# Eight experts per turn of TensorE's loop, and each upper bound loaded one expert ahead

## What is computed

```python
scores = jax.nn.sigmoid((h @ p['w_router']).astype(jnp.float32))
...
_, eidx = lax.top_k(sel, TOP_K)
wts = jnp.take_along_axis(scores, eidx, axis=-1)
wts = wts / jnp.sum(wts, axis=-1, keepdims=True) * ROUTED_SCALE
...
g = jnp.einsum('td,edf->tef', h, p['w_gate'])
u = jnp.einsum('td,edf->tef', h, p['w_up'])
a = jax.nn.silu(g) * u * comb[..., None].astype(h.dtype)
routed = jnp.einsum('tef,efd->td', a, p['w_down'])
shared = (jax.nn.silu(h @ p['w_sg']) * (h @ p['w_su'])) @ p['w_sd']
```

## Time and profile before

| what | value |
|---|---|
| time before, median of 3 runs | 1265.67 us (1260.0 to 1270.44) |
| the profiled execution, its own time | 1265.24 us |
| its span, first to last instruction | 1263.4 us |
| its mean granted clock of TensorE | 0.940 of full speed |
| TensorE busy | 1108.2 us (88%) |
| passes in the expert loop | 90, for 64 experts |
| HBM read and written | 290.26 MB, 33.82 MB |

### The profile page before, as it was taken

The page is one execution under the profiler, slowest core; times in us unless marked ns, Lnnn a source line. Parts: engine busy times, 40 slices in busy tenths (PEclk is TensorE's granted clock), DMA queues, the critical chain, the costliest instruction groups (busy, mean ns, idle before and its releaser), DMA issues.

```text
span 1263.4 us, 19646 instructions
## 1 busy us (share of the span) xinstructions
PE 1108.2 (88%) x6571; PEld 694.5 (55%) x6572; DVE 384.5 (30%) x936; ACT 334.5 (26%) x754; POOL 306.5 (24%) x500
## 2 busy tenths in 40 slices
PE   3899999988999999559999989999999989999960
PEld 1576576455666644345555555555655555555730
DVE  2200010274554223542222122222222212222687
ACT  2100100286565201312222222223222322322111
POOL 1000100101222100053343323333433333333122
PEclk9799999988897799779999999999999999999995
DMA  9811231121541001836889999997889999798652
GB/s 321 296 67 67 81 127 67 61 82 67 180 161 61 1 1 38 329 118 251 326 324 412 413 412 407 405 413 308 317 334 394 408 413 401 295 413 325 285 176 75
DMA packets 80748, 304.18 MB, mean 241 GB/s; under 512 B 13206, under 2 KB 15320, under 8 KB 63496
## 3 DMA queue, kind: packets, MB, share of 16 engines
q1 hardware_dynamic: 63800, 268.26, 54.8%
q0 software_dynamic: 16256, 33.08, 7.0%
q10 hardware_dynamic: 656, 2.36, 0.5%
HBM read 290.26 MB, written 33.82 MB: 257 GB/s over the span
## 4 chain that ended last, share of the span: by engine, by line
PE 77%; DMA 9%; DVE 7%; issue 3%; ACT 2%; POOL 1%; SPq 0%; POOLq 0%; DVEq 0%; ACTq 0%
PE bank L928 23%; PE bank L935 12%; DMA arena<-in_w_down 6%; PE bank L620 6%; PE bank L621 6%; PE bank L679 4%; PE bank L866 4%; PE bank L921 3%; PE bank L790 2%; PE bank L940 2%; PE bank L605 2%; PE bank L613 1%; DVE arena L1637 1%; PE bank L817 1%; PE bank L766 1%
## 5 line engine op out<-in xcount | busy, mean ns | idle before, releaser
L928 PE MATMUL bank<-arena 128*64 128x256 f32 x2880 | 336.1, 386 | 38.2 <-issue 22.7
L928 PEld LDWEIGHTS bank<-arena 128*64 128x64 f32 x2880 | 244.3, 139 | 162.6 <-issue 107.4
L935 PE MATMUL bank<-arena 128*64 128x512 f32 x728 | 176.3, 602 | 1.5 <-DVE arena L1594 0.6
L1600 DVE COPY arena<-bank 128x512 f32<-128x512 f32 x90 | 62.2, 692 | 365.2 <-PE bank L921 361.3
L1208 ACT COPY arena<-bank 128x128 f32<-128x128 f32 x90 | 23.9, 265 | 412.3 <-PE bank L940 412.3
L512 POOL DMA_INDIRECT arena<-h_rows,arena x93 | 98.2, 1056 | 82.7 <-POOL arena L509 78.2
L520 POOL DMA_INDIRECT y_rows<-arena x91 | 93.2, 1024 | 86.0 <-POOL arena L517 81.3
L620 PE MATMUL bank<-arena 128*128 128x288 f32 x320 | 105.2, 411 | 2.2 <-DVE arena L1287 2.2
L621 PE MATMUL bank<-arena 128*128 128x288 f32 x320 | 104.7, 409 | 0.0
L1594 DVE COPY arena<-bank 128x512 f32<-128x512 f32 x91 | 62.9, 692 | 102.0 <-PE bank L935 102.0
L935 PEld LDWEIGHTS bank<-arena 128*64 128x64 f32 x728 | 52.1, 136 | 67.1 <-issue 66.3
(11 more groups left out here) (268 smaller groups left out, 1164.7 us busy)
## 6 DMA issues: line engine op xcount, KB each, us to landing
arena<-in_w_gate SPq DMA_DIRECT2D x64, 1024.0 KB, 9.0
arena<-in_w_up SPq DMA_DIRECT2D x64, 1024.0 KB, 12.6
arena<-in_w_down SPq DMA_DIRECT2D x64, 1024.0 KB, 13.8
arena<-in_w_ada SPq DMA_DIRECT2D x12, 2048.0 KB, 8.0
arena<-in_w_in SPq DMA_DIRECT2D x6, 2048.0 KB, 9.5
arena<-y_rows SPq DMA_DIRECT2D x2, 3072.0 KB, 13.8
arena<-in_w_out SPq DMA_DIRECT2D x2, 2048.0 KB, 8.3
arena<-y_rows SPq DMA_DIRECT2D x2, 2048.0 KB, 16.0
```

Source lines behind the costliest of these rows:

```text
L928: last = pe.matmul(bank[0][n * SLOT:n * SLOT + SLOT, 0:2 * P].rearrange("p (g f) -> p g f", f=P), HGT[:, k % 4, k // 4, :], w[:, :, n * P: ...
L935: last = pe.matmul(bank[3][n * SLOT:n * SLOT + SLOT, :], AE[:, f, :], DN[j][:, f, 512 * n:512 * n + 512], start=(f == 0), stop=(f == 1))
L1600: dve.tensor_copy(hgt, bank[1][:, :]).then_inc(hgt_ready, 1)
```

## The change

The outer loop has 8 turns of eight experts in place of 16 turns of four. The four weight buffers stay (j = x % 4), and the semaphore counts that are waited for follow. `lo` and `hi` are loaded at the head of a turn only. In a turn each expert but the last loads the upper bound of the next expert, inside its first pass, between gate/up and the turn of AC; at the expert's end `lo` takes the value of `hi`, and `hi` the value loaded ahead.

```diff
-            def item(i, j, before):
+            def item(i, j, before, ahead=None):
 
                 pe.wait_ge(hgt_ready, i + 1)
                 pe.wait_ge(ac_ready, i + 1)
                 gate_up(j)
+                after = pe.value_load(START[0:1, bass.ds(ahead, 1)], min_val=1, max_val=NI) if ahead is not None else None
                 turn_out()
                 pe.wait_ge(hg_staged, i + 2)
                 pe.sem_inc(pe_mark)
...
                 down(before)
+                return after
...
-            with pe.Fori(0, NE // 4) as g:
-                e = g * 4
-                for j in range(4):
-                    lo = pe.value_load(START[0:1, bass.ds(e + j, 1)], min_val=0, max_val=NI - 1)
-                    hi = pe.value_load(START[0:1, bass.ds(e + (j + 1), 1)], min_val=1, max_val=NI)
-                    pe.wait_ge(exp_ld[j], (g + 1) * 48)
+            with pe.Fori(0, NE // 8) as g:
+                e = g * 8
+                lo = pe.value_load(START[0:1, bass.ds(e, 1)], min_val=0, max_val=NI - 1)
+                hi = pe.value_load(START[0:1, bass.ds(e + 1, 1)], min_val=1, max_val=NI)
+                for x in range(8):
+                    j = x % 4
+                    pe.wait_ge(exp_ld[j], g * 96 + (x // 4 + 1) * 48)
                     pe.sem_inc(pe_mark)
-                    item(lo, j, (j + 3) % 4)
+                    after = item(lo, j, (j + 3) % 4, e + (x + 2) if x < 7 else None)
                     with pe.If_lt(pe.to_reg(lo + 1), pe.to_reg(hi)):
                         with pe.Fori(lo + 1, hi) as i:
                             item(i, j, j)
+                    lo, hi = hi, after
```

## The result

The changed kernel takes 1333.95 us (median of 4 runs, 1326.2 to 1334.78) against 1266.34 us: ratio 1.0528, 95% interval 1.0482 to 1.0575. It is 68 us slower; the forecast was 1257 us, no change to speak of, with 1246 to 1272 as the range.

What follows compares the result with a forecast made beforehand. TensorE and the weight transfers were taken to bound the expert loop by turns. Of 26.0 us saved at boundaries 8.3 would arrive, load ahead, clock and code fetches costing nothing: 1257 us, range 1246 to 1272.

Steps and rivals of the forecast that it cites:

- What bounds the kernel: Expert loop: TensorE and the weight transfers take turns; register loads lengthen boundaries between experts.
- The two bounds: Expert loop: TensorE, and the DMA queue that brings 3 MB of weights per expert, by turns.
- the four kinds of boundary: Down to next gate/up: same expert 1.74 us; next expert after extra passes +0.31, after one pass +0.38, turn end +1.13.
- The load ahead is free: Register load behind gate/up: hidden by the sequencer's 2.2 us lead, cost zero; up to 42 us without that cover.
- How much reaches the end, 8.3 us: Boundaries in stretches not bound by transfers: 8.3 of 26.0 us arrive; 17.7 become waits for in_w_down.
- The clock term: Gate/ups at half clock after waits for weights: more possible at 1.7 us each; taken as 0, bounds 0 and +3.4.
- The size of the loop: TensorE's doubled loop body: 1,440 records, some 6 pieces, taken as held in instruction memory, so 1257 us stays.
- the first rule: TensorE's instruction memory: 128 KiB, 2,048 instructions in blocks of 256; the new body fits narrowly, sum stays 1257 us.
- The second rule of that section: TensorE's code: a taken branch out of a two-block window forces a fetch; contradicted by the 23 pieces seen before.
- Rival 3: Loop head: body of eight not held, 7 returns wait 6.9 us each; +14.4 us, 1280 us; chance 0.18.
- What would show it: Profile after: some 26 code pieces, in_w_down waits 25 to 35 us; 60 or more pieces if code is not held.

Runs made afterwards that it cites:

- before_light: Kernel before, with half of the loads of each gate and up matrix left out, all matmuls run; 1245.40 us, one run.
- carry4_light: carry4 with half of the loads of each gate and up matrix left out, all matmuls run; 1211.47 us, one run.
- carry4: Kernel before, upper bounds loaded one expert ahead, both bounds carried over turn ends in registers; 1251.21 us (0.9865), second series 1256.92 us (0.9925).
- shift8: Changed kernel with eight semaphore increments of TensorE ahead of the loop; 1260.28 us, ratio 0.9935 to the kernel before.
- shift1: Changed kernel with one semaphore increment of TensorE ahead of the loop; 1253.56 us, one run.
- pad140: Kernel before, four experts per turn, with 140 always-skipped TensorE instructions behind each expert; 1282.02 us, one run.
- eight_only: Kernel before with eight experts per turn, both bounds still loaded at each expert; 1341.21 us, ratio 1.0593.
- pad195: Kernel before, four experts per turn, with 195 always-skipped TensorE instructions behind each expert; 1594.91 us, one run.
- long40: shift8 with a never-taken branch over 40 TensorE instructions behind each of eight experts; 1299.38 us.

## Why the prediction was wrong

**What bounds the kernel.** Right. The two bounds, the four kinds of boundary, 0.31, 0.38 and 1.13 us over a floor of 1.74: before_light and carry4_light confirm their sum (35.9 us in the distances, 34 forecast for them). In the changed kernel every boundary inside a turn that has no wait for weights is at 1.74 us, but for one at 1.86.

**The load ahead is free.** Right: 1.74 us at these boundaries, and carry4's wait for issue is 0.3 us in total.

**How much reaches the end, 8.3 us.** Right for the edit, had the code been held: shift8, which is the changed kernel but for eight instructions, came out 8.2 us below before (0.9935), its loop is 597.1 us long against 605.1, and the wait for in_w_down grew to 30.0 us where I had said about 31. The clock term came out at its upper bound: four gate/ups behind such waits ran slow there in place of two, the +3.4 us that I had set at 0; they fell where the transfers are the bound.

**The size of the loop.** This is the step that failed. I called the new body "one of 1,440 records, some 6 pieces", wrote that by the first rule "the new body fits, narrowly, with the block fetched ahead", and put the cost of fetching at nothing, with 0.66 on that. What the runs show in its place: with 8 blocks in use nothing is fetched again (shift1, shift8, pad140: 25 or 26 pieces), with 9 all of it (the changed kernel, eight_only, pad195, long40: 89 to 161 pieces). TensorE's memory for code is eight blocks of 256 instructions by the Trainium skill ("Runtime: NRT & Kernel Launch", Instruction fetch mechanics), and the runs agree with that size.

Two things were wrong in my count. First, 1,440 is the number of matmuls and weight loads alone, 16 copies of 90. The waits, the branches and the register work of the sequencer lie in memory too: by the built program's count the body is 1,616 instructions, 6.3 blocks. A body of 1,440 would have touched 7 blocks at most, 8 with the one ahead, and fitted wherever it began. Second, I counted its length and not the blocks that it touches. Beginning in the last place of a block, 1,616 instructions touch 1 + 7 blocks, and with the one ahead that is 9. Beginning one place further they touch 7, and 8 with the one ahead. No trace shows the count or the place as such; that one instruction turns one case into the other (shift1) bears the place out.

The second rule of that section, a window of two blocks, was rightly set aside. With up to 8 blocks in use the runs contradict it: in shift8 the six returns after the first branch back, from the body's seventh block to its first, in 0.21 or 0.22 us, and no code is fetched for them.

**Rival 3** had the mechanism and 0.18 of the chance. Its price was too low: I took 6.9 us for a return and expected most of it to be made up elsewhere. A return costs 15.6 us on the mean against the 2.87 that a turn end costs anyway, 12.7 more, because two waits stand in a row, 7.1 and 5.9 us on the mean. And a second term was missing: after each of these stops the next gate/up ran at half the clock (1.2 GHz) for a while, 5.1 to 6.6 us long in place of 3.67. The sum by these numbers: returns 109.1 - 7 x 2.87 = +89.0; seven slow gate/ups, 41.8 - 7 x 3.67 = +16.1; other slow ones, one in place of two, -1.7; boundaries -26.0; waits for weights 6.1 - 13.8 = -7.7. That is +69.7 us, and the loop is 68.8 us longer (673.9 against 605.1). Here all 26.0 us of the boundaries are in the sum, and it still comes out within 1 us. The likely reason, which no run tests by itself: with TensorE at rest for some 95 us more, the transfers keep up (waits for weights of 6.1 us in all).

**What would show it** named the right row: "60 or more pieces and turn ends of 5 us or more". It was 89 pieces and 14 to 17 us.

## What to carry to other kernels

Before a loop of a sequencer is made longer, count the instructions of the whole body as they stand in memory, skipped ones too, and the place where the loop begins: with up to 8 blocks of 256 in use, the block ahead included, TensorE's loop turned without a fetch here. With 9, every turn fetched nine pieces again, and it was 9 to 20 us from down to gate/up at each return. The page's row for the instruction queue tells in one number whether this happens: pieces far above the program's length divided by 256. A row of matmuls and weight loads is not the whole program: here it missed 176 of 1,616 instructions, which was enough to make a body look safe. And where a loop is near the limit, a version that doesn't lengthen the body (carry4: registers carried over the turn's end) gave as much here.

## What the runs showed of the hardware that I had not expected

- One idle instruction ahead of a loop was worth 76.6 us of its length (673.9 us without it, 597.3 with it, one run), and eight were worth 74 us of the kernel's time (1333.95 against 1260.28).
- When the body is too long by one block, all of it is fetched again, not the missing block alone: 9 pieces per return in all four such kernels ((89 - 26) / 7, (90 - 27) / 7, (161 - 26) / 15).
- A fetch that the sequencer has to wait for was dear. The branch back took 6.0 to 7.9 us in the changed kernel, eight_only and long40, and up to 8.2 in pad195; the wait for the block behind the head was 5.5 to 6.3 us in the first two. Beside it ran a loop that loads weights at 330 GB/s, and no run has such a fetch without loads beside it; while the code runs in sequence, the fetches ahead are hidden (in the changed kernel the boundaries inside a turn that wait for no weights stand at 1.74 us, although six pieces come in between two stops).
- A stop of 12 us or more was each time followed by a gate/up at half the clock (1.2 GHz) for part of its length, 1.4 to 2.9 us dearer, and so was each of the 7 stops of 7.2 to 8.7 us in long40. Of the 16 waits for weights in shift8, 3.3 us at most, it was 4.
